# Prompt attention: probabilities scaled by GpSimd before their transposes, and three branches summed in one PSUM bank

## The reference

```python
p_c = _masked_softmax(s_c, (d_c >= 0)[:, None, None, :])      # compressed keys, 63 of them
o_c = jnp.einsum('tgjn,ngd->tgjd', p_c.astype(cv.dtype), cv)
...
p_s = _masked_softmax(s_s, m_s[:, :, None, :])                # selected keys: 16 blocks of 64
o_s = jnp.einsum('tgjk,tgkd->tgjd', p_s.astype(vg.dtype), vg)
...
p_w = _masked_softmax(s_w, m_w[:, None, None, :])             # window of 512 keys
o_w = jnp.einsum('tgjk,kgd->tgjd', p_w.astype(vw.dtype), vw)
o = gt[:, :, :, 0] * o_c + gt[:, :, :, 1] * o_s + gt[:, :, :, 2] * o_w
```

## Time and profile before

| | |
|---|---|
| Time, median of 3 runs | 2545.19 us (2543.06 to 2546.51) |
| Profiled execution: its time | 2545.03 us |
| Profiled execution: its span | 2543.4 us |
| Stage `attend_prompt`, first score to the end of its block | about 395.7 to 708.7 us |
| TensorE busy in 395 to 695 us | 280.44 of 300 us |
| GpSimd busy in 395 to 695 us | 1.84 of 300 us |

### The profile page before, as it was taken

How to read it: one execution, slowest core, us unless ns; L and a number is a source line. 1 busy time by engine, 2 the same in 40 slices (tenths; PEclk the granted TensorE clock), 3 DMA queues, 4 the chain that set the end, 5 groups by cost and what they waited for, 6 DMA issues and landing times. The chain is left out here.

```text
span 2543.4 us, 47485 instructions
## 1 busy us (share of the span) xinstructions
PE 2368.4 (93%) x19959; PEld 2070.9 (81%) x19959; DVE 1144.4 (45%) x2276; ACT 735.7 (29%) x1401; POOL 513.8 (20%) x377
## 2 busy tenths in 40 slices
PE   6998997999856999899989999999999999989998
PEld 3776884445534998888879999888999999989998
DVE  5532225555533445565654122355323332355665
ACT  4232124556612334222233110112111111123332
POOL 4001210000021232000012233321332323223332
PEclk8997898999976999999989999999999999999999
DMA  7335422101145141111112111241111111131221
GB/s 290 132 138 161 139 67 113 34 1 51 44 123 203 34 148 70 72 52 52 51 46 72 38 50 46 67 142 60 56 42 50 42 50 44 49 94 45 74 80 47
DMA packets 160709, 201.57 MB, mean 79 GB/s; under 512 B 14921, under 2 KB 144266, under 8 KB 156850
## 3 DMA queue, kind: packets, MB, share of 16 engines
q1 hardware_dynamic: 154866, 182.81, 22.3%
q0 software_dynamic: 5632, 15.74, 2.1%
HBM read 170.68 MB, written 31.99 MB: 80 GB/s over the span
## 5 line engine op out<-in xcount | busy, mean ns | idle before, releaser
L165 POOL CAST w_hi<-w_raw 128x1024 fp32r<-128x1024 f32 (+1 forms) x115 | 115.8, 1007 | 1300.5 <-DMA w_raw<-in_w_in 426.2
L173 PE MATMUL pP_u<-h_hi,w_hi 128*128 128x352 f32 x1056 | 340.9, 323 | 0.3 <-PEq L3044 0.3
L174 PE MATMUL pP_u<-h_lo,w_hi 128*128 128x352 f32 x1056 | 338.5, 321 | 0.0
L175 PE MATMUL pP_u<-h_hi,w_lo 128*128 128x352 f32 x1056 | 338.4, 320 | 0.0
L167 POOL TENSOR_TENSOR w_lo<-w_raw,w_hi 128x1024 fp32r<-128x1024 f32 (+1 forms) x115 | 275.5, 2396 | 9.2
L173 PEld LDWEIGHTS pP_u<-h_hi,w_hi 128*128 128x128 f32 x1056 | 198.1, 188 | 0.7 <-issue 0.6
L174 PEld LDWEIGHTS pP_u<-h_lo,w_hi 128*128 128x128 f32 x1056 | 198.5, 188 | 0.0
L175 PEld LDWEIGHTS pP_u<-h_hi,w_lo 128*128 128x128 f32 x1056 | 197.9, 187 | 0.0
L3332 DVE TENSOR_TENSOR conv<-conv,conv_sig 128x1056 f32<-128x1056 f32 x22 | 50.1, 2279 | 312.7 <-ACT conv_sig L3300 312.7
L173 PE MATMUL pP_d<-a_piece_hi,w_hi 128*128 128x352 f32 x528 | 173.4, 328 | 10.5 <-DVE a_piece_lo L3490 8.4
L3499 DVE TENSOR_TENSOR a_piece_lo<-aT,a_piece_hi 128x1408 fp32r<-128x1408 f32 (+1 forms) x71 | 135.8, 1917 | 93.0 <-ACT a_piece_hi L3428 93.0
(11 more groups left out here) (513 smaller groups left out, 5027.2 us busy)
## 6 DMA issues: line engine op xcount, KB each, us to landing
w_raw<-in_w_up SPq DMA_DIRECT2D x44, 512.0 KB, 4.1
ybT<-in_w_ada SPq DMA_DIRECT2D x9, 2048.0 KB, 8.0
w_raw<-in_w_in SPq DMA_DIRECT2D x30, 512.0 KB, 4.3
kv_ring<-in_pool_kv SPq DMA_DIRECT2D x80, 128.0 KB, 2.3
w_raw<-in_w_down SPq DMA_DIRECT2D x20, 512.0 KB, 3.5
pair_scratch<-hT SPq DMA_DIRECT2D x3, 2752.0 KB, 9.8
cx<-in_pool_c POOLq DMA_DIRECT2D x64, 128.0 KB, 3.1
cx<-in_pool_c SPq DMA_DIRECT2D x64, 128.0 KB, 3.0
```

The lines of the kernel that those rows point to most:

```text
L165: engine.tensor_copy(hi, source).then_inc(done, 1)
L173: nc.tensor.matmul(out, w_hi, x_hi, start=start, stop=False)
L174: nc.tensor.matmul(out, w_hi, x_lo, start=False, stop=False)
L175: return nc.tensor.matmul(out, w_lo, x_hi, start=False, stop=stop)
```

## The change

The division by the sum and the product with the gate are moved from the value product's output to the exponentials. "invert" (VectorE, twice for each step, four heads each) clamps and inverts the sums. GpSimd, in the order's "exp" entries, waits for the semaphore `inverted` and multiplies the 128 x keys exponentials of a head, in place, by inverse sum and gate. The transposes now wait for `scaled`, which GpSimd raises, in place of `probs`. "coef", "spread", `coef_rows`, `acc` and `part` go. The value products of the three branches of a query block add up in one bank of `pO`, and one copy for each query block ("fold", SEL alone) brings it to `ybT`. In the written order the lane of exponentials has a ninth place (the second "invert"), all lanes are pressed into nine tenths of the slot, and the value lane begins a tenth of a slot later. GpSimd's two window DMAs now stand ahead of the exponentials of step 14, and its 8 page DMAs behind its last product.

```diff
+            if prob:
+                prob[5].append(("invert", s - 1, 0))
+                prob.append([("invert", s - 1, 1)])
             lanes = [x for x in (score, prob, value) if x]
-            merged = sorted((((k + 0.5) / len(x), m, k) for m, x in enumerate(lanes) for k in range(len(x))))
+            place = lambda x, k: 0.9 * (k + 0.5) / len(x) + (0.1 if x is value else 0.0)
+            merged = sorted(((place(x, k), m, k) for m, x in enumerate(lanes) for k in range(len(x))))
...
-                pool.wait_ge(valued, last_value(free[2]))
-                for w in (1, 3):
-                    pool.dma_start(S["vw_rows"][w], A["win_v"][w].rearrange("(c p) d -> p c d", p=128)).then_inc(S["vw_in"][w], 16)
+                for e in order:
+                    if e == ("exp", free[2] + 3, 0):
+                        pool.wait_ge(valued, last_value(free[2]))
+                        for w in (1, 3):
+                            pool.dma_start(S["vw_rows"][w], A["win_v"][w].rearrange("(c p) d -> p c d", p=128)).then_inc(S["vw_in"][w], 16)
+                    if e[0] == "exp":
+                        _, n, h = e
+                        i, br = steps[n]
+                        x = held(n)[:, h, 0:extent(n)[1]]
+                        gate = 3 * h + (1, 2, 0)[br]
+                        pool.wait_ge(inverted, 2 * n + h // 4 + 1)
+                        nc.gpsimd.tensor_scalar(x, x, sums[:, n % 4, h:h + 1], S["gates"][:, i, gate:gate + 1], ALU.mult,
+                                                ALU.mult).then_inc(scaled, 1)
                 pool.wait_ge(queried, 1)
                 pool.wait_ge(scored, len(score_at))
                 load_slot(pool, "kv_pool", 0, range(1, PAGES, 2))
...
-                        pe.wait_ge(probs, prob_at[("exp", n, 4 * g + 3)] + 1)
+                        pe.wait_ge(scaled, prob_at[("exp", n, 4 * g + 3)] + 1)
...
-                    elif e[0] == "spread":
-                        t = ring(e)
-                        pe.wait_ge(coefed, n + 1)
-                        for j in range(4):
-                            for g in range(2):
-                                mm = nc.tensor.matmul(t[64 * g:64 * g + 64, 128 * j:128 * j + 128],
-                                                      coef[:, n % 4, 4 * g + j:4 * g + j + 1].broadcast_to([128, 64]), S["ident"],
-                                                      start=True, stop=True)
-                        mm.then_inc(turned, 1)
...
-                        if b == 0 and n >= 2:
-                            pe.wait_ge(folded, n - 1)
+                        turn = n // 3
+                        br = steps[n][1]
+                        if b == 0 and br == CMP and turn >= 2:
+                            pe.wait_ge(folded, turn - 1)
...
-                            mm = nc.tensor.matmul(pO[64 * g:64 * g + 64, n % 2, :], values(n, g, b),
-                                                  PT[0:w, turn_at[("turn", n, b, g)] % 6, :], start=(b == 0), stop=(b == blocks(n) - 1))
+                            mm = nc.tensor.matmul(pO[64 * g:64 * g + 64, turn % 2, :], values(n, g, b),
+                                                  PT[0:w, turn_at[("turn", n, b, g)] % 6, :], start=(br == CMP and b == 0),
+                                                  stop=(br == SEL and b == blocks(n) - 1))
...
-                        dve.wait_ge(probs, 8 * (n + 1))
-                        link(nc.vector.tensor_scalar(sums[:, n % 4, :], sums[:, n % 4, :], 1e-30, None, ALU.max))
-                        link(nc.vector.reciprocal(sums[:, n % 4, :], sums[:, n % 4, :]))
-                        kind = (1, 2, 0)[br]
-                        nc.vector.tensor_tensor(coef[:, n % 4, :], sums[:, n % 4, :], S["gates"][:, i, kind:24:3],
-                                                ALU.mult).then_inc(coefed, 1)
+                    elif e[0] == "invert":
+                        part = sums[:, n % 4, 4 * e[2]:4 * e[2] + 4]
+                        dve.wait_ge(probs, prob_at[("exp", n, 4 * e[2] + 3)] + 1)
+                        link(nc.vector.tensor_scalar(part, part, 1e-30, None, ALU.max))
+                        nc.vector.reciprocal(part, part).then_inc(inverted, 1)
...
+                        dve.wait_ge(valued, last_value(n))
+                        nc.vector.tensor_copy(S["ybT"][:, :, i * 128:i * 128 + 128],
+                                              pO[:, n // 3 % 2, :].rearrange("p (j q) -> p j q", j=4)).then_inc(folded, 1)
```

More of the change, by code:

```diff
@@ L990, in attend_prompt @@
         PT = sb("pt_p", [128, 6, 512])
-        acc, part = sb("acc_p", [128, 512]), sb("part_p", [128, 512])
-        coef_rows = sb("coef_rows", [128, 2, 512])
-        tops, bias, sums, coef = sb("tops_p", [128, 2, 8, 2]), sb("bias_p", [128, 4, 8]), sb("sums_p", [128, 4, 8]), sb("coef_p", [128, 4, 8])
+        tops, bias, sums = sb("tops_p", [128, 2, 8, 2]), sb("bias_p", [128, 4, 8]), sb("sums_p", [128, 4, 8])
         slopes = sb("slopes_p", [128, 8])
         pS, pT, pO = ps("ps_p", [128, 3, 512]), ps("pt_psum_p", [128, 3, 512]), ps("po_p", [128, 2, 512])
-        tab, ready, scored, shifted, biased, probs, turned, valued, coefed, folded, queried, chain = (
-            sem(f"ap_{n}") for n in ("tab", "ready", "scored", "shifted", "biased", "probs", "turned", "valued", "coefed", "folded", "queried",
-                                     "chain"))
+        tab, ready, scored, shifted, biased, probs, turned, valued, inverted, scaled, folded, queried, chain = (
+            sem(f"ap_{n}") for n in ("tab", "ready", "scored", "shifted", "biased", "probs", "turned", "valued", "inverted", "scaled", "folded",
+                                     "queried", "chain"))
         out = [sem(f"ap_out{n}") for n in range(3)]
@@ L1056, in attend_prompt @@
                     value.append([("turn", n, b, g) for g in range(2)] if b < nb else [])
[L1057 to L1060, removed]
                     if b >= 2:
                         value[-1].append(("value", n, b - 2))
-                value.append([("fold", n)])
+                if steps[n][1] == SEL:
+                    value.append([("fold", n)])
+            if prob:
+                prob[5].append(("invert", s - 1, 0))
+                prob.append([("invert", s - 1, 1)])
             lanes = [x for x in (score, prob, value) if x]
-            merged = sorted((((k + 0.5) / len(x), m, k) for m, x in enumerate(lanes) for k in range(len(x))))
+            place = lambda x, k: 0.9 * (k + 0.5) / len(x) + (0.1 if x is value else 0.0)
+            merged = sorted(((place(x, k), m, k) for m, x in enumerate(lanes) for k in range(len(x))))
             order += [e for _, m, k in merged for e in lanes[m][k]]
@@ L1069, in attend_prompt @@
         nth = {}
-        for kinds in (("score",), ("exp",), ("turn", "spread"), ("turn",), ("value",)):
+        for kinds in (("score",), ("exp",), ("turn",), ("value",)):
             nth[kinds] = {e: n for n, e in enumerate(e for e in order if e[0] in kinds)}
-        score_at, prob_at, ring_at, turn_at, value_at = (nth[k] for k in (("score",), ("exp",), ("turn", "spread"), ("turn",), ("value",)))
+        score_at, prob_at, turn_at, value_at = (nth[k] for k in (("score",), ("exp",), ("turn",), ("value",)))
+        ring_at = turn_at
         last_turn = lambda n: ring_at[("turn", n, blocks(n) - 1, 1)] + 1
-        by_act = lambda e: e[0] == "spread" or ring_at[e] % 3 < 2
+        by_act = lambda e: ring_at[e] % 3 < 2
         free = {3: steps.index((7, SEL)), 2: steps.index((4, SEL)), 1: steps.index((2, SEL))}
@@ L1170, in _ @@
                         if h == 0 and n >= 4:
-                            act.wait_ge(coefed, n - 3)
+                            act.wait_ge(scaled, 8 * (n - 3))
                         x = held(n)[:, h, 0:extent(n)[1]]
@@ L1181, in _ @@
                         nc.scalar.activation(PT[0:w, t % 6, :], pT[0:w, r % 3, :], ACT.Copy).then_inc(out[r % 3], 1)
[L1182 to L1187, removed]
             @block.vector
@@ L1229, in _ @@
                                                        ALU.max, ALU.mult).then_inc(biased, 1)
-                    elif e[0] == "coef":
-                        dve.wait_ge(probs, 8 * (n + 1))
-                        link(nc.vector.tensor_scalar(sums[:, n % 4, :], sums[:, n % 4, :], 1e-30, None, ALU.max))
-                        link(nc.vector.reciprocal(sums[:, n % 4, :], sums[:, n % 4, :]))
-                        kind = (1, 2, 0)[br]
-                        nc.vector.tensor_tensor(coef[:, n % 4, :], sums[:, n % 4, :], S["gates"][:, i, kind:24:3],
-                                                ALU.mult).then_inc(coefed, 1)
+                    elif e[0] == "invert":
[3 more added lines that the diff above has]
+                        nc.vector.reciprocal(part, part).then_inc(inverted, 1)
                     elif e[0] == "turn" and not by_act(e):
```

## The result

The changed kernel takes 2558.6 us (median of 7 runs, 2553.05 to 2563.91) against 2546.5 us for the kernel before on the same chips (7 runs). The ratio is 1.0045, 95% interval 1.0034 to 1.0056: slower by 0.45%, where 2554 us were forecast. The profiled execution took 2555.64 us, 10.6 us more than the one before.

What follows compares the result with a forecast made beforehand. TensorE bounds the stage, except that ScalarE's exponentials set SEL's exponential slots. 8.4 (SEL) + 3 (WINB) - 6.7 ("coef") + 4.1 (end) = +8.8 us on 2545.0, so 2554 us; range 2526 to 2596.

Steps and rivals of the forecast that it cites:

- What goes: On TensorE, 24 spreads (24.5 us) and waits for "coef" (6.7 us) vanish: 31.2 us, the most that can be won.
- the spread of SEL: In the slot with SEL's values, which TensorE fills, removing this spread was to give 1.0 us back.
- The product's price: GpSimd's multiplication of one head: cast plus a fifth, 1.24 us for 1024 keys down to 0.34 for 128.
- The slow product: Rival: GpSimd's product takes 2.4 us for 1024 keys, +51 us, 2596; shares chance 0.20 with uncovered waits.
- The handover: SEL's exponentials to transposes through VectorE's invert and four GpSimd products: 4p - 2.1 per query block, sum +8.4 us.
- in the SEL handovers above all: Sign to look for: TensorE idle 25 us or more before its transposes, released by GpSimd, mostly at SEL steps.
- 8.3 us: SEL handovers of the query blocks i = 7 to 4, forecast at 2.9, 2.3, 1.8 and 1.3 us.
- 0.1 + 3 - 6.7 = -3.6 us: Later, smaller steps: remaining SEL handovers, WINB's +3 in the three smallest query blocks, and the vanished "coef" waits, -6.7.
- The handover of WINB: WINB's exponentials to transposes: TensorE late by 2.1 us, covered except in the three smallest query blocks, +3 us.
- 3.0 us of slack cover it: In the slot with SEL's exponentials, ScalarE fills 13.24 of 14.60 us, TensorE 11.6, so WINB's lateness costs nothing.
- The end of the stage: GpSimd's eight page DMAs now stand behind its last product: block end 712.8 in place of 708.7, +4.1 us.
- The faster one: Rival: handover hidden, spreads' time comes through; 27 us at most (2518), centre 2532; chance of faster 0.28.

Runs made afterwards that it cites:

- e11_no_product_old_order: Changed kernel without GpSimd's products and the inverts (division and gates left out), lanes placed as before the change: 2511.6 us, ratio 0.9860.
- e3: Changed kernel with four inverts of two heads in place of two of four, leaving two products behind the last: 2540.1 us, ratio 0.9982.
- e6: Changed kernel with the value lane 0.3 of a slot behind instead of 0.1, lanes pressed to 0.7: 2540.0 us, ratio 0.9980.
- e12: Changed kernel, products kept, with the lanes placed as before the change (exponentials still in nine places): 2604.4 us, ratio 1.0236.
- e5_fill_wait: Changed kernel with 16 unneeded identity transposes ahead of TensorE's second wait for GpSimd in each WINB and SEL step's first block: 2551.7 us, ratio 1.0029.
- e1_no_product: Changed kernel without GpSimd's products and the inverts, in the new lane order; division and gates left out: 2506.1 us, ratio 0.9839.
- e4_pages_split: Changed kernel with four of GpSimd's eight page DMAs at the stage's end moved to SyncE: 2554.5 us, ratio 1.0036.
- e7_pairs_fill: Changed kernel with inverts of two heads and 10 filling transposes ahead of TensorE's waits for GpSimd: 2536.9 us, ratio 0.9974.
- e8_product_twice: Changed kernel with GpSimd multiplying in two passes, by inverse sums, then by gates, 384 products in all: 2877.9 us, ratio 1.1313.

## Why the prediction was right, point by point

**What goes: right in its sum, wrong in its place.** 31.2 us forecast, 32.2 measured at the stage's end in the old order. But I wrote that the spread of SEL, "in the slot that TensorE fills, gives 1.0 us back", and that in the slots that ScalarE holds a spread gives nothing besides 0.5 us. It was the reverse: 24.30 to 24.44 there, 15.80 to 11.64 here (24.5 and 11.7 in the old order). The row that says so stood in front of me: ScalarE was idle for 29.7 us ahead of its copies of the spreads. Its idle time ahead of all its copies was 60.8 us before and is 40.2 in e11_no_product_old_order. An engine that holds a slot and waits in it, in its own order, for a copy, gets back the wait, not only the copy. Another 9.5 us of the stage came from the lanes' new order, which I had priced at nothing.

**The product's price: right.** 1.20 us for 1024 keys where 1.24 was taken; 0.45 for 128 where 0.34 was. The cast's slope per column (0.84 ns) held, the fixed part is twice the cast's (0.345 us against 0.18). All products together are 124 us instead of 113. The slow product did not happen.

**The handover: the cause was right, single terms were off.** TensorE waits 35.4 us for GpSimd where I asked for 25 or more. It does not lie "in the SEL handovers above all", though: 13.6 us are SEL's, 17.9 WINB's and 3.9 CMP's. For SEL, i = 7 to 4, it is 2.5, 2.1, 1.6 and 0.9 us. Each cut or stretch of the handover moved the time as it should (e3, e6, e12). Up to the bias of step 13, all of i = 7 to 4, I had 8.3 us; the marks are 605.51 and 608.86, 3.35 us. From there to the last bias (695.53 and 701.37) I had 0.1 + 3 - 6.7 = -3.6 us; it was +2.5. Up to step 13 the four slots with SEL's values are together 10.2 us longer than before and the four with SEL's exponentials 1.4, but the four with SEL's scores are 8.3 us shorter; I had given that slot 1 us each. The smaller steps were worse than forecast: behind that mark TensorE waits 16.4 us for GpSimd, where it had waited 6.7 for "coef" and 3.1 for exponentials.

**The handover of WINB: this step failed.** "3.0 us of slack cover it" is wrong. The wait came (2.85 us where 2.1 was forecast), and nothing covered it: ScalarE's exponentials stand behind its copy of the late transpose, 1.86 us of idle time, and TensorE's clock fell for the next 7 us or so. The slot took 15.72 us where it had taken 14.60, and 11.39 without products. Slack on one engine is no cover when the engine that it waits for has a place in its own queue.

**The clock: left out.** Neither the sum nor a rival had it. Over the stage the granted clock is 0.91 against 0.97 of the kernel before, and e5_fill_wait shows that keeping TensorE busy in the wait wins more than its work costs. Against e1_no_product it is 20.8 us of TensorE's time, more than a third of the 53.5 us between the two stage ends.

**The end of the stage: larger on its own, less in the time.** From the last bias to the next block it was 13.2 us and is 19.2: 6.0 where 4.1 was forecast, mostly for the 2.9 us instead of 0.8 from the last instruction, now GpSimd's DMA, to the next block. But e4_pages_split took 3.8 us of it away and the following stage gave them back.

3.35 + 2.5 + 6.0 = 11.8 us at the stage's end within rounding, less 1.2 in the stage behind: 10.6, where the sum said 8.8. The total is as close as it is by luck in part, because an under-counted gain (41.7 us, shown by e1_no_product) and an under-counted cost (53.5 us from there to the changed kernel) cancel.

**The rivals.** The faster one asked that the four products fit into what TensorE has left; with pairs they nearly do and the kernel is faster, but by 5 us (e3_invert_pairs) or 7 to 8 (e7_pairs_fill), not 27. VectorE's queue was a small matter: its inverts waited 6.3 us for ScalarE in all. The slow product's rival holds a slip: it sets WINB's 6.2 us of products against the slack, where the forecast set the lateness, which would be 2.1 + 2.8 = 4.9 us; that gives +15 in place of +25 and 2585 us in place of 2596.

## What to carry to other kernels

Moving an operation off the busiest engine can cost more than it wins when its new place is between two engines that hand work over in each step. Price the handover by what is left behind the last signal (here four heads, then two), and make that piece small before anything else; add what a stall does to the engines that queue behind it and to TensorE's clock. And look for gains where an engine that holds a stretch is idle in its own order, not where the engine relieved of work is busy.

## What was unexpected of the hardware

- GpSimd multiplies by two columns of scalars in 1200 ns for 128 x 1024, and by one column, with no second operation, in 2843 ns: 0.835 against 2.50 ns per column. For 1024 columns the form with less to do is more than twice as slow (e8_product_twice).
- How long TensorE had been idle does not by itself tell whether the granted clock falls. Around the idle stretches of 2.8 to 3.2 us at the four large WINB handovers it fell to 0.50. At SEL handovers it stayed at 1.00 behind 2.5 and 2.1 us (444.7 and 498.6), but fell at 549 behind 1.6 us (547.8). In the kernel before, it was 0.50 from 430 to 432, behind an idle stretch of 1.57 us that ended at 428.9.
- VectorE's bias instruction on 8 columns, 0.16 us alone, took up to 0.82 us beside GpSimd's products.
